# Layer 0 attention: who turns the first four heads' probabilities, and who scales k and v of the second four heads

## The chip, the cores and the metric

The kernel runs on one core of a Trainium2 chip. The metric is the device time of one execution in microseconds; three runs of the kernel before gave 2122.54, 2122.59 and 2122.71 us, median 2122.59.

Engines are named as in the profile: PE is TensorE's matmuls and PEld its weight loads, DVE is VectorE, ACT is ScalarE, POOL is GpSimd, SP is SyncE, which issues the loads from memory.

## The reference, cut to what matters

A decoder trunk of two layers over 256 tokens with a model width of 2048. Layer 0 projects the normalised input in one product to u, va, q, k and v. One half of the mixer is a gated unit with a 128x128 position mixing, the other is dilated attention with 8 heads of 128. Both halves go through one output projection. Then comes a squared-ReLU MLP; layer 1 is stick-breaking attention with 16 heads, and another MLP.

The dilated attention has three branches (window, dilation) = (128, 1), (512, 4), (2048, 16), merged by their softmax denominators:

```
s = q . k - slope(head) * distance          (causal)
p = exp(s - max(s)) * count(distance)       count = number of branches that hold this key
o = (p / sum(p)) @ v
```

With 256 tokens this is, for each head, a lower-triangular score matrix in three 128x128 blocks (queries 0-127 with keys 0-127, queries 128-255 with keys 0-127, queries 128-255 with keys 128-255).

## The kernel before

**Units and ticks.** Every large product is cut into 94 units. A unit is a product of all 256 tokens (two blocks of 128) with 512 columns of a weight matrix, over a depth of 2048: 8 ticks of two 128-deep steps each. For precision every weight is split into w_hi and w_lo and every activation likewise, so a step is three products, and a tick is 12 matmuls of 128x512 (L1203, from tick_tokens). Units 4 to 6 give q, k and v of layer 0's heads 0 to 3 (the first group), units 7 to 9 those of heads 4 to 7 (the second group), units 10 to 13 are the output projection.

**Rings.** w_raw holds the 8 ticks of a unit as they come from memory in four quarters of 1 MB. w_hi and w_lo are rings of 4 ticks. ACT makes w_hi of a tick (L394) when PE is done with the tick four before; DVE makes w_lo (L723) when w_hi is there; PE starts the tick when w_lo is there. SP issues the load of a quarter when w_lo of the ticks that lay in it is made.

**The order of the other work.** It is written out by hand. For ACT and DVE a unit is a loop over positions t = 1 to 7 and a last one: the extras of t, then the conversion of the tick four later; behind position 7 comes post (the evacuation of the unit's result), then the extras of 8 and the conversion. For PE the extras of t run ahead of tick t. Over the three units of a q, k, v group t runs from 0 to 24, and in the output projection from 0 again. Each engine executes its own list strictly in order.

**Attention of a group.** post on DVE scales q, k and v out of PSUM by the row norms (L975, scaled), into q_tok (the memory of kT), k_tok (the memory of y_sb) and v_sb; DVE turns q into qT by 16 block operations of 32x256 at the positions of TURNS_L0, and k into kT at those of TURNS_K (L829). PE's scores follow at the start of the next unit. Then, inside the next group of units: DVE adds the distances (L890), takes the maximum (t = 1, L899) and subtracts it (t = 2, L905), ACT takes the exponential (t = 3, L518), DVE multiplies by the counts (t = 4, L909) and normalises (t = 5, L914 to L918). What is left is zs, 4 heads x 384 columns, with queries on the partitions.

The values product needs the keys on the partitions, so zs has to be turned into tmp:
- first group (during units 7 to 9): at t = 8 PE transposes 12 blocks of 128x128 into PSUM (l0_pT, L1431), ACT copies them to tmp in two pieces (l0_copy_pT, L523), and PE multiplies tmp with v_sb at t = 10 (values);
- second group (during units 10 to 13): DVE turns zs in 16 block operations of 32x384, four at each of t = 6 to 9 (turn_p, L928), and PE's values run at t = 13.

After the values, ACT makes hid_hi (L527) and DVE hid_lo (L934) out of PSUM, for the output projection. PE's scores of the second group, at t = 24, wait for both and for the turned k. Semaphores: s_pn counts normalised halves, s_pT and s_pc the transposes and their copies, s_pturned the end of turn_p, s_o the values, post_done the evacuated units; PE starts unit u when units 0 to u-2 are evacuated.

Of the kernel before, what the change touches and what calls it, by code (L numbers as in the profile page):

```python
# [32 lines left out]
ACT = mybir.ActivationFunctionType  # L33
AX = mybir.AxisListType

P = 128
T = 256
TB = T // P
# [19 lines left out]
HG = 4  # L58
# [5 lines left out]
TRI = 3 * P  # L64
# [20 lines left out]

TURNS_GATE = {9: 3, 11: 2, 13: 3, 14: 4, 15: 4}
TURNS_L0 = {11: 4, 12: 4, 13: 4, 14: 4}
TURNS_L1 = {9: 2, 10: 2, 11: 4, 12: 2, 13: 4, 14: 2}
TURNS_K = {17: 4, 18: 4, 19: 4, 20: 4}

# [16 lines left out]
def trunk_kernel(nc, x_in, pre_mix, post_mix, pre_ffn, post_ffn, ab_w_in, ln_g, ln_b, sgu_w, sgu_b,  # L107
                 ab_w_out, sb_w_in, sb_w_out, ffn_w1, ffn_w2, shapes, out):
    ctx = ExitStack()
    with ctx:  # L110
# [3 lines left out]
        def sem(name):  # L114
            return ctx.enter_context(nc.semaphore(name))
# [33 lines left out]
        ident = cst[:, 0:P]  # L149
# [78 lines left out]
        s_sm = sem("s_sm")  # L228
        s_ex = sem("s_ex")
        s_pn = sem("s_pn")  # L230
        s_pT = sem("s_pT")
        s_pc = sem("s_pc")
        s_pturned = sem("s_pturned")
        s_wturned = sem("s_wturned")
        s_ab = sem("s_ab")
# [148 lines left out]
        def _(act):  # L384
# [19 lines left out]
            def unit(u, post, extras=None, first=1):  # L404

                for t in range(first, TICKS):
                    for f in (extras or {}).get(t, []):
                        f()
                    conv_at(u, t)
                post()  # L410
                for f in (extras or {}).get(TICKS, []):
                    f()
                if not (isinstance(u, int) and u == UNITS - 1):
                    conv(u + 1, 4)
# [101 lines left out]
            def l0_exp(grp):  # L516
                act.wait_ge(s_sm, 4 * grp + 4)
                nc.scalar.activation(zs[:, :, :], zs[:, :, :], ACT.Exp).then_inc(s_ex, 1)  # L518

            def l0_copy_pT(n):  # L520
                act.wait_ge(s_pT, n + 1)
                b = 2 * (n % 2)
                nc.scalar.activation(tmp[:, b:b + 2, :], ps[:, 4 + b:6 + b, 0:TRI], ACT.Copy).then_inc(s_pc, 1)  # L523

            def o_hi(n, b, tile):
                act.wait_ge(s_o, n + 1)
                nc.scalar.activation(hid_hi[:, bass.ds(tile, 2), :],  # L527
                                     ps[:, 6 + b, :].rearrange("p (h t) -> p h t", t=T), ACT.Copy).then_inc(s_ohi, 1)

            def l0_extras(grp):  # L530
                copies = {8: [lambda: l0_copy_pT(2 * grp), lambda: l0_copy_pT(2 * grp + 1)]} if grp == 0 else {}
                return {3: [lambda: l0_exp(grp)], **copies,
                        (10, 13)[grp]: [lambda: o_hi(2 * grp, 0, 8 + 4 * grp), lambda: o_hi(2 * grp + 1, 1, 8 + 4 * grp + 2)]}


            def l1_logs(b, grp):
# [23 lines left out]
                        13: [lambda: l1_weights(1, grp)],  # L560
                        15: [lambda: o_hi(2 * grp + 4, 0, 4 * grp), lambda: o_hi(2 * grp + 5, 1, 4 * grp + 2)]}

            def qkv_group(u, extras):
                for i in range(3):
                    unit(u + i, nothing, {t - 8 * i: f for t, f in extras.items() if 8 * i < t <= 8 * i + 8})

            def sum_squares_psum(u0, c):

# [120 lines left out]
            for j in range(2):  # L689
                unit(2 + j, lambda j=j: gelu_u(j))  # L690
            qkv_group(4, {t: [lambda m=m: gate_hi(m)] for m, t in enumerate(GATE_HI)})
            qkv_group(7, l0_extras(0))
            out_phase(U_OUT0, l0_extras(1), 1)
            ffn(U_FFN0, 0)

# [14 lines left out]
        def _(dve):  # L710
# [33 lines left out]
            def unit_finished(u):  # L744
                dve.wait_ge(pe_ticks, 8 * u + 8)
# [86 lines left out]
            def turns(plan, dst, src):  # L832

                at, extras = 0, {}
                for t, n in plan.items():
                    extras[t] = [lambda a=at, n=n: turn(dst, src, range(a, a + n))]
                    at += n
                return extras

            def merged(*plans):  # L840
                every = {}
                for plan in plans:
                    for t, f in plan.items():
                        every[t] = every.get(t, []) + f
                return every
# [41 lines left out]
            def l0_scores(h, head):  # L887
                dve.wait_ge(s_sc, head + 1)
                dve.wait_ge(s_cst, 16)
                nc.vector.scalar_tensor_tensor(zs[:, h, :], far_c, -(2.0 ** -(head + 1)), ps[:, 4 + h, 0:TRI],  # L890
                                               ALU.mult, ALU.add).then_inc(s_zs, 1)
# [25 lines left out]
                    m = rden[:, i, :].unsqueeze(2).broadcast_to([P, HG, z.shape[2]])  # L917
                    nc.vector.tensor_tensor(z, z, m, ALU.mult).then_inc(s_pn, 1)  # L918

            def turn_p(first):  # L920

                if first == 0:
                    dve.wait_ge(s_pn, 4)
                for n in range(first, first + 4):
                    q4, k4 = n // 4, n % 4
                    rows = zs[32 * q4:32 * q4 + 32, :, :].rearrange("p h (c k f) -> p (h c) k f", c=3, k=4)
                    cols = tmp[32 * k4:32 * k4 + 32, :, :].rearrange("p h (c q t) -> p (h c) q t", c=3, q=4)
                    last = nc.vector.transpose(cols[:, :, q4, :], rows[:, :, k4, :])  # L928
                if first == 12:
                    last.then_inc(s_pturned, 1)  # L930

            def o_lo(n, b, tile):
                dve.wait_ge(s_ohi, n + 1)
                nc.vector.tensor_tensor(hid_lo[:, bass.ds(tile, 2), :], ps[:, 6 + b, :].rearrange("p (h t) -> p h t", t=T),  # L934
                                        hid_hi[:, bass.ds(tile, 2), :].bitcast(F32), ALU.subtract).then_inc(s_olo, 1)

            def l0_extras(grp):
                return {1: [lambda: l0_max(grp)], 2: [lambda: l0_less_max(grp)], 4: [lambda: l0_count(grp)],
                        5: [lambda: l0_normalise(grp)],
                        **({t: [lambda t=t: turn_p(4 * t - 24)] for t in range(6, 10)} if grp else {}),  # L940
                        (10, 13)[grp]: [lambda: o_lo(2 * grp, 0, 8 + 4 * grp), lambda: o_lo(2 * grp + 1, 1, 8 + 4 * grp + 2)]}


            def l1_scores(h, grp):
# [22 lines left out]
                        12: [lambda: l1_exponent(1, grp)],  # L967
                        15: [lambda: o_lo(2 * grp + 4, 0, 4 * grp), lambda: o_lo(2 * grp + 5, 1, 4 * grp + 2)]}

            def qkv_group(u, extras, q_plan, scores):  # L970
                def scaled(i, dst, factor=None):

                    unit_finished(u + i)
                    for b in range(TB):
                        last = nc.vector.tensor_scalar(dst[:, b, :], ps[:, 2 * ((u + i) % 2) + b, :], rst[:, 6 + b:7 + b], factor,  # L975
                                                       ALU.mult, *(() if factor is None else (ALU.mult,)))
                    last.then_inc(post_done, 1)
                    if i < 2:
                        dve.wait_ge(post_done, u + (i + 1))

                k_turns = turns(TURNS_K, kT, k_tok)
                k_turns[20] = [lambda: turn(kT, k_tok, range(12, 16)).then_inc(s_turned, 1)]
                extras = merged(extras, turns(q_plan, qT, q_tok), k_turns,
                                {24: [lambda h=h: scores(h) for h in range(HG)]})
                for i, post in enumerate((lambda: scaled(0, q_tok, SCALE), lambda: scaled(1, k_tok),
                                          lambda: scaled(2, v_sb))):
                    unit(u + i, post, {t - 8 * i: f for t, f in extras.items() if 8 * i < t <= 8 * i + 8})
# [197 lines left out]
            gates = merged({t: [lambda m=m: gate(m)] for m, t in enumerate(GATE)},  # L1185
                           {t: [lambda m=m: gate_lo(m)] for m, t in enumerate(GATE_LO)})
            qkv_group(4, merged(turns_u(1), gates), TURNS_GATE, lambda h: l0_scores(h, h))
            qkv_group(7, l0_extras(0), TURNS_L0, lambda h: l0_scores(h, 4 + h))
            out_phase(U_OUT0, l0_extras(1), 1)
            ffn(U_FFN0, 0)  # L1190

# [9 lines left out]
        def _(pe):  # L1201
# [214 lines left out]
            def l0_scores(grp):  # L1416

                pe.wait_ge(s_turned, grp + 1)
                if grp == 0:
                    pe.wait_ge(s_sgt, 4)  # L1420
                else:
                    pe.wait_ge(s_olo, 2)
                for h in range(HG):
                    mm(ps[:, 4 + h, 0:P], qT[:, h, 0:P], kT[:, h, 0:P], True, True)
                    mm(ps[:, 4 + h, P:TRI], qT[:, h, P:T], kT[:, h, :], True, True).then_inc(s_sc, 1)

            def l0_pT(grp):
                pe.wait_ge(s_pn, 2 * grp + 2)
                for h in range(HG):
                    for c in range(3):  # L1430
                        last = nc.tensor.transpose(ps[:, 4 + h, c * P:(c + 1) * P], zs[:, h, c * P:(c + 1) * P], ident)  # L1431
                    if h % 2:
                        last.then_inc(s_pT, 1)

            def values(b, w):

                for i in range(2):
# [3 lines left out]
                last.then_inc(s_o, 1)  # L1441

            def l0_values(grp):
                pe.wait_ge(*((s_pc, 2), (s_pturned, 1))[grp])
                for b in range(2):
                    values(b, tmp[:, 2 * b:2 * b + 2, :])

            def l0_extras(grp):
                return {0: [lambda: l0_scores(grp)], **({} if grp else {8: [lambda: l0_pT(grp)]}),
                        (10, 13)[grp]: [lambda: l0_values(grp)]}  # L1450

            def l1_scores(grp):

# [159 lines left out]
```

## Time and profile before

| | |
|---|---|
| median of three runs | 2122.59 us |
| the profiled execution's own time | 2122.69 us |
| its span | 2120.7 us |
| PE busy | 2111.2 us |
| DVE busy | 1481.2 us |
| ACT busy | 1028.1 us |
| mean granted clock of TensorE | 0.999 |

The span is from the first to the last recorded instruction of one execution; 2.0 us of the execution's time lie around it. Matmuls are pipelined, so durations of PE rows overlap: the step from one start to the next is the time that a matmul costs, not its own duration. In a timeline row the first number is the start, the second the time covered by the instructions that the row merges.

### The profile page before, as it was taken

The numbers are of one execution on the slowest core, as the hardware profiler recorded it, in microseconds if no ns is written. First come the engines' busy times: TensorE is split into PE (matmuls) and PEld (weight loads), VectorE is DVE, ScalarE is ACT, GpSimd is POOL, SyncE is SP. The second block draws the span as 40 slices with busy tenths as digits, with TensorE's granted clock in tenths as the row PEclk, the third lists the DMA queues.
The fourth block names the chain that finished last, engine by engine and source line by source line (L and its number), as shares of the span: only waits on it lengthen the run. The fifth ranks groups of instructions, "written<-read, shape, count | busy, mean of one in ns | idle before, by whom it ended". The sixth has DMA issues, their size and how long they took to land.

```text
span 2120.7 us, 25442 instructions
## 1 busy us (share of the span) xinstructions
PE 2111.2 (100%) x9448; PEld 1748.5 (82%) x9448; DVE 1481.2 (70%) x1924; ACT 1028.1 (48%) x1180; POOL 20.1 (1%) x24
## 2 busy tenths in 40 slices
PE   9999999999999999999999999999999999999998
PEld 7888888888888888888888888888888888888886
DVE  6797867764774775586778778577746855764875
ACT  6444346543543453454645554665434544544553
POOL 0000001000000000000000000000000000000000
PEclk9999999999999999999999999999999999999999
DMA  9655555656656656655555555456556566656553
GB/s 323 207 179 171 191 193 170 206 195 187 195 199 190 186 198 218 184 193 198 178 179 178 179 178 199 160 160 216 199 186 192 180 213 182 198 197 214 183 199 119
DMA packets 204077, 406.81 MB, mean 192 GB/s; under 512 B 6544, under 2 KB 9936, under 8 KB 203472
## 3 DMA queue, kind: packets, MB, share of 16 engines
q1 hardware_dynamic: 203712, 405.37, 58.3%
q8 instruction: 63, 1.03, 0.2%
q14 instruction: 30, 0.25, 0.0%
q10 hardware_dynamic: 272, 0.16, 0.0%
HBM read 403.41 MB, written 2.10 MB: 191 GB/s over the span
## 4 chain that ended last, share of the span: by engine, by line
PE 99%; DVE 0%; DVEq 0%; ACT 0%; issue 0%; POOL 0%; POOLq 0%
PE ps L1203 99%; PE ps L1352 1%; DVE x_sb L767 0%; PE ps L1431 0%; DVE act_pair L1111 0%; DVE act_pair L773 0%; ACT tmp L497 0%; DVE y_sb L1081 0%; DVEq L110 0%; DVE w_lo L800 0%; PE ps L1257 0%; POOL rs_bc L350 0%; PE ps L1545 0%; PE ps L1550 0%; DVE rst L856 0%
## 5 line engine op out<-in xcount | busy, mean ns | idle before, releaser
L723 DVE TENSOR_TENSOR w_lo<-w_raw,w_hi 128x1024 fp32r<-128x1024 f32 x750 | 910.7, 1225 | 561.9 <-ACT w_hi L394 558.2
L394 ACT ACTIVATE w_hi<-w_raw 128x1024 fp32r<-128x1024 f32 x750 | 789.9, 1061 | 897.0 <-PE ps L1203 893.2
L1203 PE MATMUL ps<-w_hi,act_pair 128*128 128x512 f32 x3456 | 1072.0, 390 | 0.4 <-ACT w_hi L457 0.3
L1203 PEld LDWEIGHTS ps<-w_hi,act_pair 128*128 128x128 f32 x3456 | 647.1, 188 | 136.2 <-issue 2.0
L1203 PE MATMUL ps<-w_lo,act_pair 128*128 128x512 f32 x1728 | 670.2, 390 | 0.0
L1203 PE MATMUL ps<-w_hi,hid_hi 128*128 128x512 f32 x1280 | 498.7, 390 | 0.0
L1203 PE MATMUL ps<-w_hi,hid_lo 128*128 128x512 f32 x1280 | 498.0, 389 | 0.0
L1203 PE MATMUL ps<-w_lo,hid_hi 128*128 128x512 f32 x1280 | 498.0, 389 | 0.0
L1203 PEld LDWEIGHTS ps<-w_lo,act_pair 128*128 128x128 f32 x1728 | 324.1, 188 | 66.6 <-DVE w_lo L800 0.4
L829 DVE STREAM_TRANSPOSE qT<-kT 32x256 f32<-32x256 f32 x608 | 265.0, 436 | 42.2 <-ACT kT L605 32.8
L1203 PEld LDWEIGHTS ps<-w_hi,hid_lo 128*128 128x128 f32 x1280 | 240.2, 188 | 50.0
L1203 PEld LDWEIGHTS ps<-w_hi,hid_hi 128*128 128x128 f32 x1280 | 240.3, 188 | 49.7
L1203 PEld LDWEIGHTS ps<-w_lo,hid_hi 128*128 128x128 f32 x1280 | 240.3, 188 | 49.5
L610 ACT ACTIVATE hid_hi<-qT 128x512 fp32r<-128x512 f32 x64 | 37.0, 627 | 124.2 <-DVE qT L829 124.2
L829 DVE STREAM_TRANSPOSE kT<-y_sb 32x256 f32<-32x256 f32 x96 | 41.8, 435 | 1.6
L1033 DVE TENSOR_TENSOR hid_lo<-qT,hid_hi 128x512 fp32r<-128x512 f32 x64 | 41.2, 685 | 0.0
L601 ACT ACTIVATE qT<-ps,rst 128x512 f32<-128x512 f32 x64 | 40.1, 676 | 0.0
L605 ACT ACTIVATE kT<-qT 128x1024 f32<-128x1024 f32 x32 | 34.0, 1062 | 1.0
L425 ACT ACTIVATE act_pair<-ps,gpre 128x256 fp32r<-128x256 f32 (+1 forms) x80 | 28.3, 450 | 8.2 <-PE ps L1352 8.1
L364 POOL TENSOR_TENSOR rst<-rst,neg_half 128x1 f32<-128x1 f32 (+1 forms) x13 | 11.1, 855 | 2093.3 <-DVE rst L856 1994.8
L773 DVE SCALAR_TENSOR_TENSOR act_pair<-ps,gpre,act_pair 128x256 fp32r<-128x256 f32 (+1 forms) x70 | 28.2, 460 | 1.5 <-ACT act_pair L425 1.3
L497 ACT ACTIVATE tmp<-ps 128x512 f32<-128x512 f32 x20 | 11.9, 593 | 30.7 <-PE ps L1203 22.8
(104 smaller groups left out, 474.3 us busy)
## 6 DMA issues: line engine op xcount, KB each, us to landing
w_raw<-in_ffn_w_dram SPq DMA_DIRECT2D x256, 1024.0 KB, 5.3
w_raw<-in_sb_w_in_dram SPq DMA_DIRECT2D x48, 1024.0 KB, 5.1
w_raw<-in_ab_w_in_dram SPq DMA_DIRECT2D x36, 1024.0 KB, 5.2
w_raw<-in_ab_w_out_dram SPq DMA_DIRECT2D x16, 1024.0 KB, 5.0
w_raw<-in_sb_w_out_dram SPq DMA_DIRECT2D x16, 1024.0 KB, 5.0
w_raw<-in_ab_w_in_dram SPq DMA_DIRECT2D x6, 512.0 KB, 8.5
x_sb<-in_x_dram SPq DMA_DIRECT2D x8, 256.0 KB, 7.2
gpost<-in_norm_post_mix_dram SPq DMA_DIRECT2D x2, 1024.0 KB, 7.9
```

The lines of the kernel that those rows point to most:

```text
L394: nc.scalar.activation(w_hi[:, t % RING, :, :], w_raw[:, t // 2, h:h + 2, :], ACT.Copy).then_inc(hi_ready, 1)
L425: last = nc.scalar.activation(act_hi[:, kt, part], ps[:, x_bank(k, j), i * T + part.start:i * T + part.stop], ACT.Copy, scale=gpre[:, k * ...
L497: nc.scalar.activation(junk[:, 2 * NC:3 * NC], src, ACT.Square, accum_out=ssy[:, b, c:c + 1]).then_inc(s_ssy, 1)
L601: last = nc.scalar.activation(relu_tok[:, b, :], ps[:, 2 * (j % 2) + b, :], ACT.Relu, scale=rst[:, 6 + b:7 + b])
L605: nc.scalar.activation(sq_tok, relu_tok, ACT.Square).then_inc(f_sq, 1)
L610: nc.scalar.activation(hid_hi[:, 4 * j + i:4 * j + i + 2, :], sq_T[:, i:i + 2, :], ACT.Copy).then_inc(f_hi, 1)
L723: nc.vector.tensor_tensor(w_lo[:, t % RING, :, :], w_raw[:, t // 2, h:h + 2, :], w_hi[:, t % RING, :, :].bitcast(F32), ALU.subtract).then_ ...
L773: last = nc.vector.scalar_tensor_tensor(act_lo[:, kt, part], ps[:, x_bank(k, i if k == 0 and j == 0 else j), i * T + part.start:i * T + pa ...
L829: last = nc.vector.transpose(cols[:, :, :, tp, :], rows[:, :, :, fq, :])
L1033: nc.vector.tensor_tensor(hid_lo[:, tiles, :], sq_T[:, i:i + 2, :], hid_hi[:, tiles, :].bitcast(F32), ALU.subtract).then_inc(done, 1)
L1203: return nc.tensor.matmul(dst, lhsT, rhs, start=start, stop=stop, skip_group_check=True)
L1352: last = nc.tensor.transpose(ps[:, x_bank(k, j), i * T + b * P:i * T + (b + 1) * P], x_sb[:, b, kt * P:(kt + 1) * P], ident)
```

## The change

For the first group the PE transposes, the ACT copies and their two semaphores are gone. DVE's turn_p gets the group as an argument and does the job in both groups: in the first with two block operations at each of t = 6 to 13. PE's values, ACT's hid_hi and DVE's hid_lo of the first group move from t = 10 to t = 15.

The turns of the second group's q move with it: before, four at each of t = 11 to 14; now two at 11 and 12 and four at 13, 14 and 15, and DVE waits for the end of the last.

k and v of the second group (units 8 and 9) are scaled out of PSUM by ACT instead of DVE, two activations of 128x512 each. DVE waits at its own place of post for k only. q stays with DVE, and so do all three in the other groups.

```diff
+TURNS_L0_LATE = {11: 2, 12: 2, 13: 4, 14: 4, 15: 4}
+VALUES_L0 = (15, 13)
...
 ACT
-            def l0_copy_pT(n):
-                act.wait_ge(s_pT, n + 1)
-                b = 2 * (n % 2)
-                nc.scalar.activation(tmp[:, b:b + 2, :], ps[:, 4 + b:6 + b, 0:TRI], ACT.Copy).then_inc(s_pc, 1)
...
+            def scaled(u, dst):
+                unit_finished(u)
+                act.wait_ge(post_done, u)
+                for b in range(TB):
+                    last = nc.scalar.activation(dst[:, b, :], ps[:, 2 * (u % 2) + b, :], ACT.Copy, scale=rst[:, 6 + b:7 + b])
+                last.then_inc(post_done, 1)
...
-            qkv_group(7, l0_extras(0))
+            qkv_group(7, l0_extras(0), (nothing, lambda: scaled(8, k_tok), lambda: scaled(9, v_sb)))
...
 DVE
-            def turn_p(first):
+            def turn_p(grp, first, end):
                 if first == 0:
-                    dve.wait_ge(s_pn, 4)
-                for n in range(first, first + 4):
+                    dve.wait_ge(s_pn, 2 * grp + 2)
+                for n in range(first, end):
...
-                        **({t: [lambda t=t: turn_p(4 * t - 24)] for t in range(6, 10)} if grp else {}),
-                        (10, 13)[grp]: [lambda: o_lo(...), lambda: o_lo(...)]}
+                        **({t: [lambda t=t: turn_p(1, 4 * t - 24, 4 * t - 20)] for t in range(6, 10)} if grp else
+                           {t: [lambda t=t: turn_p(0, 2 * t - 12, 2 * t - 10)] for t in range(6, 14)}),
+                        VALUES_L0[grp]: [lambda: o_lo(...), lambda: o_lo(...)]}
...
+                    if i in by_act:
+                        if i < 2:
+                            dve.wait_ge(post_done, u + (i + 1))
+                        return
...
+                if by_act:
+                    q_turns[15] = [lambda: chain(turn(qT, q_tok, range(12, 16)))]
...
-            qkv_group(7, l0_extras(0), TURNS_L0, lambda h: l0_scores(h, 4 + h))
+            qkv_group(7, l0_extras(0), TURNS_L0_LATE, lambda h: l0_scores(h, 4 + h), (1, 2))
...
 PE
-            def l0_pT(grp):
-                pe.wait_ge(s_pn, 2 * grp + 2)
-                for h in range(HG):
-                    for c in range(3):
-                        last = nc.tensor.transpose(ps[:, 4 + h, c * P:(c + 1) * P], zs[:, h, c * P:(c + 1) * P], ident)
-                    if h % 2:
-                        last.then_inc(s_pT, 1)
...
             def l0_values(grp):
-                pe.wait_ge(*((s_pc, 2), (s_pturned, 1))[grp])
+                pe.wait_ge(s_pturned, grp + 1)
...
-                return {0: [lambda: l0_scores(grp)], **({} if grp else {8: [lambda: l0_pT(grp)]}),
-                        (10, 13)[grp]: [lambda: l0_values(grp)]}
+                return {0: [lambda: l0_scores(grp)],
+                        VALUES_L0[grp]: [lambda: l0_values(grp)]}
```

## Rows read from the trace of the kernel before

**Rows 1.** The page's part 1: busy us, share of the span, instructions.

```profile
PE 2111.2 (100%) x9448; PEld 1748.5 (82%) x9448; DVE 1481.2 (70%) x1924; ACT 1028.1 (48%) x1180; POOL 20.1 (1%) x24
```

**Rows 2.** The chain that ended last: start us, us, what.

```profile
45.74 145.22 PE ps L1203 x660
190.95 1.31 PE ps L1431 x12
192.26 137.15 PE ps L1203 x618
```

**Rows 3.** Timeline of PE and PEld, 189 to 201: start us, us, instruction.

```profile
190.79 1.47 PE L1431 MATMUL ps<-cst,zs 128*128 128x128 f32 x12
192.02 0.48 PE L1203 MATMUL ps<-w_hi,act_pair 128*128 128x512 f32 x1
192.10 0.19 PEld L1203 LDWEIGHTS ps<-w_lo,act_pair 128*128 128x128 f32 x1
...
197.59 2.78 PE L1203 MATMUL ps<-tmp,v_sb 128*128 128x256 f32 x16
200.13 0.48 PE L1203 MATMUL ps<-w_hi,act_pair 128*128 128x512 f32 x1
```

**Rows 4.** Timeline of ACT, 191 to 218, with idle time before and releaser.

```profile
191.05 1.06 ACT L394 ACTIVATE w_hi<-w_raw 128x1024 fp32r<-128x1024 f32 x1 [1.66 <-PE ps L1203]
...
205.92 1.06 ACT L394 ACTIVATE w_hi<-w_raw 128x1024 fp32r<-128x1024 f32 x1 [1.66 <-PE ps L1203]
208.64 1.06 ACT L394 ACTIVATE w_hi<-w_raw 128x1024 fp32r<-128x1024 f32 x1 [1.66 <-PE ps L1203]
...
216.80 1.06 ACT L394 ACTIVATE w_hi<-w_raw 128x1024 fp32r<-128x1024 f32 x1 [1.66 <-PE ps L1203]
```

**Rows 5.** Timeline of DVE, 190 to 211.

```profile
190.31 3.49 DVE L723 TENSOR_TENSOR w_lo<-w_raw,w_hi 128x1024 fp32r<-128x1024 f32 x3
193.72 1.41 DVE L975 TENSOR_SCALAR kT<-ps,rst 128x512 f32<-128x512 f32 x2
...
205.44 1.77 DVE L829 STREAM_TRANSPOSE qT<-kT 32x256 f32<-32x256 f32 x4
...
208.48 1.78 DVE L829 STREAM_TRANSPOSE qT<-kT 32x256 f32<-32x256 f32 x4
```

**Rows 6.** One line's instructions, ACT: a scaled activation, min/median/max ns.

```profile
L601 ACT ACTIVATE qT<-ps,rst x64: 671/677/682, 357.6 to 2027.3; 128x512 f32<-128x512 f32 x64
```

**Rows 7.** Timeline of DVE, 264 to 276, and the line's min/median/max ns.

```profile
264.81 1.23 DVE L723 TENSOR_TENSOR w_lo<-w_raw,w_hi 128x1024 fp32r<-128x1024 f32 x1
266.07 2.31 DVE L928 STREAM_TRANSPOSE tmp<-zs 32x384 f32<-32x384 f32 x4
...
273.24 2.33 DVE L928 STREAM_TRANSPOSE tmp<-zs 32x384 f32<-32x384 f32 x4
...
L928 DVE STREAM_TRANSPOSE tmp<-zs x16: 560/570/574, 262.5 to 275.0; 32x384 f32<-32x384 f32 x16
```

**Rows 8.** Timeline of the opening, 1 to 7.

```profile
1.17 2.93 PE L1203 MATMUL ps<-rs_bc 128*128 128x256 f32 x6 [1.17 <-POOL rs_bc L350]
...
5.59 0.68 DVE L800 TENSOR_TENSOR w_lo<-w_raw,w_hi 128x512 fp32r<-128x512 f32 x1
6.33 0.30 PEld L1203 LDWEIGHTS ps<-w_lo,act_pair 128*128 128x128 f32 x2 [0.41 <-DVE w_lo L800]
```

**Rows 9.** Timeline of DVE at the start of unit 10.

```profile
245.01 1.23 DVE L723 TENSOR_TENSOR w_lo<-w_raw,w_hi 128x1024 fp32r<-128x1024 f32 x1 [0.96 <-ACT w_hi L394]
```

**Rows 10.** Timeline of PE, the second group's values.

```profile
276.30 2.78 PE L1203 MATMUL ps<-tmp,v_sb 128*128 128x256 f32 x16
```

**Rows 11.** DMA issues: count, KB each, median us from issue to landing.

```profile
w_raw<-in_ab_w_in_dram SPq DMA_DIRECT2D x36, 1024.0 KB, 5.2
```

**Rows 12.** Stretches after the last matmul: busy us by engine, PEclk, DMA share, GB/s.

```profile
2112.90:2117.00 4.10, 0.00 (x0) 0.00 (x0) 3.32 (x7) 0.52 (x2) 0.54 (x1) 1.00 0.32 132
2117.00:2120.70 3.70, 0.00 (x0) 0.00 (x0) 0.36 (x1) 0.00 (x0) 0.00 (x0) 0.50 0.69 256
```

More of the change, by code:

```diff
@@ L230, in trunk_kernel @@
         s_pn = sem("s_pn")
-        s_pT = sem("s_pT")
-        s_pc = sem("s_pc")
         s_pturned = sem("s_pturned")
@@ L530, in l0_extras @@
             def l0_extras(grp):
-                copies = {8: [lambda: l0_copy_pT(2 * grp), lambda: l0_copy_pT(2 * grp + 1)]} if grp == 0 else {}
-                return {3: [lambda: l0_exp(grp)], **copies,
-                        (10, 13)[grp]: [lambda: o_hi(2 * grp, 0, 8 + 4 * grp), lambda: o_hi(2 * grp + 1, 1, 8 + 4 * grp + 2)]}
+                return {3: [lambda: l0_exp(grp)],
+                        VALUES_L0[grp]: [lambda: o_hi(2 * grp, 0, 8 + 4 * grp), lambda: o_hi(2 * grp + 1, 1, 8 + 4 * grp + 2)]}
             def l1_logs(b, grp):
@@ L561, in l1_extras, with qkv_group @@
                         15: [lambda: o_hi(2 * grp + 4, 0, 4 * grp), lambda: o_hi(2 * grp + 5, 1, 4 * grp + 2)]}
-            def qkv_group(u, extras):
+            def scaled(u, dst):
[4 more added lines that the diff above has]
+                last.then_inc(post_done, 1)
+            def qkv_group(u, extras, posts=(nothing, nothing, nothing)):
                 for i in range(3):
-                    unit(u + i, nothing, {t - 8 * i: f for t, f in extras.items() if 8 * i < t <= 8 * i + 8})
+                    unit(u + i, posts[i], {t - 8 * i: f for t, f in extras.items() if 8 * i < t <= 8 * i + 8})
             def sum_squares_psum(u0, c):
@@ L928, in turn_p @@
                     last = nc.vector.transpose(cols[:, :, q4, :], rows[:, :, k4, :])
-                if first == 12:
+                if end == 16:
                     last.then_inc(s_pturned, 1)
@@ L939, in l0_extras @@
                         5: [lambda: l0_normalise(grp)],
-                        **({t: [lambda t=t: turn_p(4 * t - 24)] for t in range(6, 10)} if grp else {}),
-                        (10, 13)[grp]: [lambda: o_lo(2 * grp, 0, 8 + 4 * grp), lambda: o_lo(2 * grp + 1, 1, 8 + 4 * grp + 2)]}
+                        **({t: [lambda t=t: turn_p(1, 4 * t - 24, 4 * t - 20)] for t in range(6, 10)} if grp else
+                           {t: [lambda t=t: turn_p(0, 2 * t - 12, 2 * t - 10)] for t in range(6, 14)}),
+                        VALUES_L0[grp]: [lambda: o_lo(2 * grp, 0, 8 + 4 * grp), lambda: o_lo(2 * grp + 1, 1, 8 + 4 * grp + 2)]}
             def l1_scores(h, grp):
@@ L968, in l1_extras, with qkv_group @@
                         15: [lambda: o_lo(2 * grp + 4, 0, 4 * grp), lambda: o_lo(2 * grp + 5, 1, 4 * grp + 2)]}
-            def qkv_group(u, extras, q_plan, scores):
+            def qkv_group(u, extras, q_plan, scores, by_act=()):
                 def scaled(i, dst, factor=None):
+                    if i in by_act:
+                        if i < 2:
+                            dve.wait_ge(post_done, u + (i + 1))
+                        return
                     unit_finished(u + i)
@@ L982, in qkv_group @@
                 k_turns[20] = [lambda: turn(kT, k_tok, range(12, 16)).then_inc(s_turned, 1)]
-                extras = merged(extras, turns(q_plan, qT, q_tok), k_turns,
+                q_turns = turns(q_plan, qT, q_tok)
+                if by_act:
+                    q_turns[15] = [lambda: chain(turn(qT, q_tok, range(12, 16)))]
+                extras = merged(extras, q_turns, k_turns,
                                 {24: [lambda h=h: scores(h) for h in range(HG)]})
```

## The prediction

> **What bounds the kernel now.** I read the page's busy shares first: PE is busy 2111.2 us of a span of 2120.7 us, VectorE (DVE) 70%, ScalarE (ACT) 48% [rows 1]. Then the chain of waits. It is PE nearly from end to end, and around the change it is 145.22 us of matmuls, then the twelve transposes for 1.31 us, then 137.15 us of matmuls, with no wait between them [rows 2]. So any time that PE spends or loses in this stretch moves the end one for one, and what DVE and ACT do costs nothing as long as PE never waits for it. The last view is the timeline of each engine around 190 us, for how early DVE is with what PE needs next.
>
> I count ticks of the second group (heads 4 to 7 being projected) from 0. PE ends tick 7 at 190.79, turns the probabilities, does ticks 8 and 9, and starts the values products at 197.59 [rows 3]. A tick is 2.72 us: the starts of ACT's conversions, each released by the end of a tick, lie that far apart [rows 4]. DVE's work is in one strict order of positions: before position t come the extras of t, then the conversion of w_lo for tick t+4. It came out of the normalising late: position 5's conversion starts at 190.31, and those of 5, 6 and 7 run back to back [rows 5], though the last of their three w_hi had been there since 192.11 [rows 4] and the others a tick and two earlier. DVE therefore starts the changed stretch with a backlog.
>
> **What goes from PE.** The transposes hold PE 190.79 to 192.02. The two ticks behind them take until 197.59, that is 5.57 us where two at the usual pace are 5.44 us. Without them the values products' old place comes at 190.79 + 5.44 = 196.23 instead of 197.59: 1.36 us less. ACT loses the two copies of tmp; it waits 1.66 us for PE in a tick anyway [rows 4], so this is worth nothing.
>
> **What DVE gets, and when PE needs it.** Sixteen block transposes of 32x384, two ahead of each position 6 to 13, and the values wait for the last. The same operation on the same tiles stands in the next group: four take 2.31 to 2.33 us, 0.58 us each, and the conversion behind takes 1.26 us until the next transpose [rows 7]. The other pieces: a conversion followed by something else 1.14 us, the scaling of q 1.41 us plus some 0.06 us for the wait on itself, four turns of q with the conversion behind them 3.04 us, so 1.78 us for four turns [rows 5]. DVE's queue from 190.31 to the last transpose:
> - eight conversions (positions 5 to 12): two at 1.14 (5 and 7) and six at 1.26, 9.8 us
> - the scaling of q: 1.5 us
> - sixteen transposes: 9.3 us
> - the two plus two turns of q planned at 11 and 12: 1.8 us
>
> Together 22.4 us: the last transpose ends at 212.7. Nothing in this list waits for ACT or PE: the conversion of position 8 would start at 198.8, and its w_hi is there by 194.8 (tick 8 ends 193.51, and ACT needs 1.3 us); each later one has more room.
>
> PE, undisturbed, ends tick 14 at 190.79 + 7 x 2.72 = 209.83 and stands before the values of position 15. It is released at 212.7 + 0.06: in the opening a load of weights starts 0.06 us after the DVE instruction it waits for [rows 8]. The first load of weights is then not hidden behind a matmul: two in a row took 0.30 us, one shows as 0.19 us [rows 3, 8], so the next step comes after 0.11 us; I put 0.1 us for it (0 to 0.2). **PE stands still for 3.0 us** (2.7 to 3.3 with the pieces' scatter), in a place where it now never does.
>
> Ticks up to 14 don't wait first. PE needs w_lo of tick 12 at 201.67 and it is ready at 200.1; of tick 13 at 204.39, ready 202.5; of tick 14 at 207.11, ready 204.9; margins 1.6, 1.9 and 2.2 us. And if one of them did fail, that wait would come out of the later one, since the release of the values hangs on DVE's queue alone.
>
> **Behind the stall.** Values 2.54 us as now, then tick 15 ends at 218.2 (now 216.5, from ACT's conversion at 216.80 [rows 4]). Queued on DVE behind the last transpose: four turns of q, conversion 13 (done 215.7; tick 17 wants it at 220.9), four turns, conversion 14 (done 218.7, wanted 223.7), the two hid_lo and four turns with the wait on itself, conversion 15 (done 223.1, wanted 226.4). DVE catches up while PE stands.
>
> ACT's scaling of k costs two activations; the same form elsewhere is 677 ns [rows 6], so k_tok is there some 2.7 us after tick 15, at 220.9. DVE, which waits for it before position 16, gets there at 223.1: no time. Behind DVE's wait stand the k turns and conversion 16; the k turns end near 235.3, and the scores need them at 239.9. ACT has 1.66 us a tick free and nothing of PE's next three ticks hangs on it. The scaling of v goes the same way; DVE loses 1.4 us of it, then waits for ACT's conversion anyway, as it does now at 245.01, where the idle time before it is 0.96 us [rows 9]. So the second group's values, whose last transpose now ends 0.7 us before PE asks (275.57 against 276.30 [rows 7, 10]), keep that margin: both move with PE. I cost both scalings at nothing; if that cover failed they would cost up to 1.4 us each. SP's load for ticks T and T+1 is released by the w_lo of tick T-7, made at position T-11, and ACT wants it at position T-4: 7 x 2.72 = 19 us, against 5.2 us to land [rows 11]; a DVE that is some 5 us late leaves that room. The wait after the last turns of q is a wait of DVE on itself of 0.06 us, under the same cover.
>
> **The sum.** -1.36 + 3.0 = +1.6 us. The profiled execution took 2122.69 us, 0.10 above the median of the runs, so 2122.59 + 1.6 = 2124.2 us.
>
> **Two rules of the Trainium skill.** By the rows, a transpose costs PE 0.11 us (1.31 us for twelve), and DVE 9.3 us for the whole job. "VectorE: DVE Perf Modes", section "Rules for kernel authors", says to turn 128x128 blocks on TensorE if a PSUM destination will do, which speaks against this change. In its section "The three transpose paths" a TensorE transpose is 390 ns; by that the change would free 4.7 us of PE and end 1.7 us faster. No chance goes to that result: the rows price these very transposes, pipelined at 0.11 us, and the forecast comes out on the rule's side for another reason, DVE's backlog.
>
> At the end, in the stretch from 2112.9 on in which no matmul runs, the granted clock holds 1.00 for 4.1 us and is 0.50 after that: from 2.4 to 1.2 GHz [rows 12]. "TensorE: Matmul & The Clock Gate", section "What's actually happening", has the low level as the default, which activity releases. The trace agrees; whether 3.0 us of standing still is enough for it, no row shows. It is the first rival.
>
> **Rivals.**
> 1. The stall also lowers the clock. For: PE stops for 3 us, which it nowhere does between its first ticks and its last. Against: the clock held for 4.1 us at the end. If it fell for the values and nothing more, their 2.54 us would double, 2126.7 us; with the tick behind them too, 2129.5 us. A row with such a price is the opening, where six matmuls of 256 columns took 2.93 us, 0.49 us each [rows 8]; in the values, eight of 128 and eight of 256 columns in 2.54 us, one of 256 is some 0.21 us.
> 2. The other side: DVE is in time, PE doesn't wait, and the whole 1.36 us stay: 2121.2 us. Its place is the release of the values at 209.8. The queue would have to fit 19.5 us instead of 22.4, so a transpose would have to cost 0.40 us instead of 0.58; from 0.49 us down the change is no loss. Against it: all sixteen in the trace took 560 to 574 ns [rows 7], and even the smaller 32x256 turns 0.44 us.
> 3. A second wait behind the first: DVE, with the twelve turns and two hid_lo ahead of the k turns, is late with conversion 14 or 15, or with the k turns. The margins are 5.0, 3.3 and 4.6 us, so it needs an unseen delay of over 3 us; a loss of 1 to 2 us on top, 2125.7 us.
> 4. That the change doesn't do what it says: if the compiled order kept DVE's work elsewhere, the transposes would still be gone from PE, and it is the second rival's time.
>
> **How the numbers follow.** Forecast (stall at full clock) 0.76, own range 2123.7 to 2124.8; lower clock 0.10; no or less stall than gain 0.09; second wait 0.05. The range from 2121.2 to 2126.0 takes in the forecast, the second wait and the no-stall case, and leaves out the lower clock. What a measurement of this kernel tells from no change is 0.2%, 4.2 us. Slower by more than that means above 2126.8: half of the first rival and a little of the third, 0.06. Faster by that, below 2118.3, no case gives: 0.01. Same: 0.93.
>
> **What would show it.** In the changed trace PE idles once, for some 3 us, just before the products of tmp and v_sb near 210 us, with DVE's transpose named as the releaser; DVE is busy without a gap from 190.3 to 212.7; tick 14 ends at 209.8; the granted clock is 1.00 throughout; there is no other PE idle time, and everything behind lies 1.6 us later than now. I am wrong if PE's idle time there is under 1.3 us, if w_lo holds PE at tick 12 to 14, or if the clock column drops behind the stall.

## The result

Over seven runs each the changed kernel takes 2130.7 us (2129.09 to 2131.19) and the kernel before 2122.71 us (2122.49 to 2123.16); the ratio is 1.0035, 95% interval 1.0025 to 1.0045. It is slower by 8.0 us where 1.6 were forecast, and the time lies outside the range. The profiled execution took 2130.98 us, span 2129.0 us, mean granted clock 0.997.

The runs fall into two groups: three from 2129.1 to 2129.6 us with a mean clock of 0.998, four from 2130.7 to 2131.2 us with 0.997. The distance, some 1.5 us, is about what one of the two low clocks below costs; that the three runs had one of them and not both is inferred, since one execution alone was traced.

The page's busy row, and its row of the queue that loads instructions (packets, MB, share of time). In the kernel before that queue has 63 packets and 1.03 MB.

```profile
PE 2113.9 (99%) x9436; PEld 1750.2 (82%) x9436; DVE 1487.3 (70%) x1936; ACT 1027.4 (48%) x1182; POOL 20.0 (1%) x24
q8 instruction: 72, 1.18, 0.2%
```

PE's waits: engine, who released it, us in total, times, longest.

```profile
PE ps L1213 <- issue: 2.9, 1, 2.9
PE ps L1213 <- DVE tmp L930: 2.7, 1, 2.7
PE ps L1213 <- POOL rs_bc L350: 1.2, 1, 1.2
PE ps L1213 <- DVE w_lo L802: 0.2, 1, 0.2
```

The wait for tmp is the forecast one. The first row was in no forecast: PE stood still for 2.9 us and, by the profile, waited for nobody. Where each lies, in the timelines of DVE around 212 and of PE around 212 and in the MLP of layer 1:

```profile
211.83 1.16 DVE L930 STREAM_TRANSPOSE tmp<-zs 32x384 f32<-32x384 f32 x2
213.02 1.78 DVE L831 STREAM_TRANSPOSE qT<-kT 32x256 f32<-32x256 f32 x4
```

```profile
209.93 0.39 PE L1213 MATMUL ps<-w_hi,act_pair 128*128 128x512 f32 x1
213.05 4.55 PE L1213 MATMUL ps<-tmp,v_sb 128*128 128x256 f32 x16 [2.73 <-DVE tmp L930]
217.35 0.48 PE L1213 MATMUL ps<-w_hi,act_pair 128*128 128x512 f32 x1
...
1767.99 0.42 PE L1213 MATMUL ps<-w_hi,act_pair 128*128 128x512 f32 x1
...
1769.17 0.40 PE L1213 MATMUL ps<-w_hi,act_pair 128*128 128x512 f32 x1
1772.48 0.39 PE L1213 MATMUL ps<-w_hi,act_pair 128*128 128x512 f32 x1 [2.92 <-issue]
```

The values products are issued over 213.05 to 217.35, 4.30 us where the kernel before has 2.54 [rows 3]. The stretches around both stops say why; the column behind POOL is the granted clock, as a share of 2.4 GHz.

```profile
210.50:213.00 2.50, 0.00 (x0) 0.00 (x0) 2.44 (x4) 0.97 (x1) 0.00 (x0) 1.00 1.02 388
213.00:216.40 3.40, 3.35 (x10) 2.90 (x11) 3.29 (x6) 0.39 (x1) 0.00 (x0) 0.51 0.73 308
216.40:220.00 3.60, 3.60 (x20) 3.08 (x19) 3.54 (x7) 0.81 (x2) 0.00 (x0) 0.99 0.73 244
1769.60:1772.40 2.80, 0.00 (x0) 0.00 (x0) 0.96 (x1) 0.00 (x0) 0.00 (x0) 1.00 0.41 92
1772.90:1776.30 3.40, 3.40 (x9) 2.62 (x9) 0.34 (x1) 1.06 (x1) 0.00 (x0) 0.51 0.75 272
```

In the 3.4 us behind each stop the clock is at 0.51, the lower of its two levels (1.2 of 2.4 GHz), and PE loses about half of that. So the 8.3 us between the two profiled executions are, term by term: -1.36 for the transposes; +0.33 for the opening (the end of tick 14 is at 210.16 instead of 209.83; the same point of the opening, the small transpose near 45 us, moves by up to 0.9 us from kernel to kernel, 45.46 to 46.33 us in the ten traces without padding at the start); +2.9 for the wait; +1.75 for the slow values; +2.92 for the second stop; +1.7 for its low clock. The sum is 8.2.

### The profile page after: what moved, and what is told of

Same layout as the page of the kernel before. It is cut to its first block, busy times and chain, and to the rows that moved or that the text cites. A ratio compares the mean times of both kernels' runs of the same rounds, so it can differ in the third digit from the quotient of the medians.

```text
span 2129.0 us, 25434 instructions
## 1 busy us (share of the span) xinstructions
PE 2113.9 (99%) x9436; PEld 1750.2 (82%) x9436; DVE 1487.3 (70%) x1936; ACT 1027.4 (48%) x1182; POOL 20.0 (1%) x24
## 4 chain that ended last, share of the span: by engine, by line
PE 96%; DVE 2%; SPq 1%; DMA 1%; issue 0%; ACT 0%; DVEq 0%; ACTq 0%
PE ps L1213 96%; DVE w_lo L725 1%; DMA w_raw<-in_ab_w_in_dram 1%; PE ps L1362 1%; DVE tmp L930 0%; SPq L309 0%; SPq L299 0%; SPq L322 0%; ACT w_hi L394 0%; DVE x_sb L769 0%; DVE den L916 0%; DVE zs L920 0%; SPq L304 0%; DVE qT L831 0%; DVE zs L911 0%
```

## The experiments

Two things had to be explained. For the first stop: is the low clock a consequence of PE's standing still? For the second, some words on the code ahead. Each layer's MLP is written with a loop (`pe.Fori`), whose body of some 1,600 PE instructions runs twice from the same place of PE's instruction stream; `1767.99` above is the first matmul of the second pass in layer 1. Theory A was that the place of a loop in PE's instruction stream decides, because the change took 24 PE instructions out ahead of it; the rival was anything else that the change shifted in time. The kernel before gave 2122.70 us beside the first four kernels (31 runs, 2122.47 to 2123.84) and 2122.84 us beside the next four (27 runs, 2122.37 to 2123.61).

**pad24**: the stream behind 213 us back at its old place.

```diff
             def l0_values(grp):
+                if grp == 0:
+                    for _ in range(24):
+                        pe.sem_inc(s_pad, 1)
                 pe.wait_ge(s_pturned, grp + 1)
```

> The changed kernel, with 24 semaphore increments (of a semaphore that nobody reads) in PE's stream just ahead of the first group's wait for the turned probabilities. They run inside that wait, and every PE instruction behind them lies at the same place of the stream as in the kernel before (the change took 24 instructions out: 12 loads of weights and 12 matmuls). Theory A (PE's second stop, 2.92 us at 1769.6 with nothing waited for, comes from where the MLP loop of layer 1 lies in PE's instruction stream): that stop is gone, and the low clock behind it; what is left is -1.36 + 2.9 + 1.7 (clock behind the first stop) + up to 0.3, 2126.0 to 2126.3 us, and PE idles only at 210 to 213. Rival (the stop comes from something else that the change shifted, such as transfers or the other engines' code): still 2129.1 to 2131.2 us with the stop near 1769.6.

2125.95 us in the median of ten runs. PE's waits, the page's row of the instruction queue, and the clock behind the stop:

```profile
PE ps L1214 <- DVE tmp L931: 2.7, 1, 2.7
PE ps L1214 <- POOL rs_bc L351: 1.2, 1, 1.2
PE ps L1214 <- DVE w_lo L726: 0.2, 1, 0.2
```

```profile
q8 instruction: 63, 1.03, 0.2%
```

```profile
213.00:216.40 3.40, 3.19 (x12) 2.77 (x13) 3.28 (x7) 0.60 (x1) 0.00 (x0) 0.64 0.82 342
216.40:220.00 3.60, 3.60 (x17) 2.98 (x17) 3.54 (x7) 0.60 (x1) 0.00 (x0) 0.86 0.66 242
```

The second stop and the nine additional instruction loads are gone; 4.75 us come back with them. What is left of the change is the first stop, and the runs differ in their clock: three at 2124.5 to 2124.8 us with a mean clock of 0.999, five at 2125.6 to 2126.3 with 0.998, two at 2127.2 and 2127.3 with 0.997. The traced execution is one of the five, and in it the low clock is seen; for the others it is inferred from time and mean clock. So the same stop of 2.7 us lowers the clock in most executions and not in all. The last two lose some 2.6 us against the first three, more than the 1.75 us that were traced, and neither was traced.

**filler**: PE has matmuls to do while it waits.

```diff
+                if grp == 0:
+                    for _ in range(12):
+                        mm(ps[:, 6, :], act_pair[:, 0, 0, 0:P], act_pair[:, 0, :, :], True, True)
                 pe.wait_ge(s_pturned, grp + 1)
```

> The changed kernel, with 12 matmuls of 128x512 into an unused PSUM bank ahead of the same wait: 12 x 0.227 = 2.7 us of PE work where it otherwise stands still, and again 24 instructions, so the stream behind lies as before. Theory A: PE's wait shrinks to some 0.2 us, the values products start at the same 213.0, the granted clock stays 1.00, no stop near 1769: 2122.7 - 1.36 + 2.9 = 2124.3 us (to 2124.6), 1.7 us less than pad24. Rival (the clock falls whatever PE does there, or the slow values products have another cause): the same as pad24, 2126.

2124.41 us, and all ten runs between 2124.12 and 2124.98. PE's timeline, and the stretches as above:

```profile
210.55 2.88 PE L1213 MATMUL ps<-act_pair 128*128 128x512 f32 x12
213.45 2.89 PE L1213 MATMUL ps<-tmp,v_sb 128*128 128x256 f32 x16
```

```profile
210.50:213.00 2.50, 2.50 (x12) 2.07 (x12) 2.43 (x5) 1.06 (x1) 0.00 (x0) 1.00 0.93 323
213.00:216.40 3.40, 3.38 (x19) 2.71 (x19) 3.31 (x6) 0.63 (x2) 0.00 (x0) 1.00 0.91 374
```

DVE is as late as before and the values start no earlier, but the clock stays at 1.00 and the time is 1.5 us below pad24's median. The 12 matmuls also put the stream behind them back at its old place, as in pad24, and no second stop appears (63 packets). So the 1.5 us are the price of the clock alone, and the low clock is a consequence of PE having nothing to do.

**values17**: the wait removed by asking later.

```diff
-VALUES_L0 = (15, 13)
+VALUES_L0 = (17, 13)
```

> The changed kernel with the first group's values, hid_hi and hid_lo at t = 17 instead of 15. PE comes there two ticks later, at about 215.5, and the last transpose is over at 213.0. Theory A: no wait there and no low clock there; the transposes' 1.36 us are gained; the stop in the MLP of layer 1 stays (2.9 us, and 1.7 us of low clock behind it in some executions): 2124.3 to 2126.0 us. Rival (that stop comes from the timing of transfers or other engines, which shifts here by over 4 us): 2121.3 us.

2125.99 us (2123.96 to 2126.43). PE's waits no longer have tmp in them; the second stop is as long as it was, though it lies 5 us earlier. Behind this stop, too, the clock falls in some executions only: three runs take 2124.0 to 2124.7 us with a mean clock of 0.999 (the traced one is among them and holds 1.00 there), seven 2125.7 to 2126.4 us with 0.998. Its waits and its instruction queue:

```profile
PE ps L1213 <- issue: 2.9, 1, 2.9
PE ps L1213 <- POOL rs_bc L350: 1.2, 1, 1.2
PE ps L1213 <- DVE w_lo L802: 0.3, 1, 0.3
```

```profile
q8 instruction: 72, 1.18, 0.2%
```

**no_transposes**: the kernel before, and only PE's stream shorter.

```diff
-                for h in range(HG):
-                    for c in range(3):
-                        last = nc.tensor.transpose(...)
-                    if h % 2:
-                        last.then_inc(s_pT, 1)
+                for h in range(2):
+                    pe.sem_inc(s_pT, 1)
```

> The kernel before without the 12 transposes on PE (two semaphore increments in their place; ACT copies what lies in PSUM, so the first group's probabilities are left out of the result). DVE, ACT and all places are as before; only PE's stream is 23 instructions shorter behind 190 us. Theory A: the transposes' 1.36 us are gained, and the stop in the MLP of layer 1 appears: 2122.7 - 1.36 + 2.9 = 2124.3 us, 2126.0 where the clock falls behind it. Rival: 2121.3 us and no stop.

2125.96 us (2124.42 to 2126.89): with PE work taken away and everything else in its place, the kernel, which leaves the first group's probabilities out of its result, is 3.3 us slower. The timeline at the stop:

```profile
1764.22 0.19 PEld L1203 LDWEIGHTS ps<-w_hi,act_pair 128*128 128x128 f32 x1
1764.44 0.39 PE L1203 MATMUL ps<-w_hi,act_pair 128*128 128x512 f32 x1
1767.58 0.19 PEld L1203 LDWEIGHTS ps<-w_hi,act_pair 128*128 128x128 f32 x1 [3.18 <-issue]
1767.59 0.50 PE L1203 MATMUL ps<-w_hi,act_pair 128*128 128x512 f32 x1 [2.75 <-issue]
```

The instruction queue has 72 packets again. Here the seventh load of weights of the loop's pass waits; in the changed kernel, whose stream is one instruction shorter here, the seventh load had run and its matmul waited. Counted in the compiled stream, both are instruction 13043.

**values17_pad8**: is it that place?

```diff
+                if grp == 0:
+                    for _ in range(8):
+                        pe.sem_inc(s_pad, 1)
```

> As values17, with 8 increments ahead of the values. Counted in the compiled stream of PE, the stop so far came in front of one and the same instruction, number 13043: the matmul of the seventh product behind the loop's start in the changed kernel, and the load of weights of the seventh in no_transposes, whose stream is one instruction longer. With 8 more, number 13043 is the matmul of the third product. Theory A, fixed place of the stream: the stop of 2.9 us now comes behind two matmuls of the loop's second pass, not behind six. Rival (the stop hangs on the loop's start, or on time): behind six matmuls, or no stop. Time 2124 to 2127 us either way with a stop.

2127.77 us, one run. The timeline:

```profile
1763.89 0.40 PE L1214 MATMUL ps<-w_hi,act_pair 128*128 128x512 f32 x1
1764.13 0.40 PE L1214 MATMUL ps<-w_lo,act_pair 128*128 128x512 f32 x1
1764.13 0.19 PEld L1214 LDWEIGHTS ps<-w_hi,act_pair 128*128 128x128 f32 x1
...
1768.29 0.62 PE L1214 MATMUL ps<-w_hi,act_pair 128*128 128x512 f32 x2 [3.76 <-issue]
```

Two matmuls and the third load run, the third matmul waits: number 13043 again. The stop is longer, 3.8 us, where 2.9 were expected. The rows say why: PE goes on 4.4 us behind the pass's first matmul (1763.89 to 1768.29) here and 4.5 us behind it in the changed kernel (1767.99 to 1772.48), so with two products ahead of the place instead of six less work lies inside that time. In both traces a packet of the instruction queue starts 2.1 to 2.2 us behind the pass's first matmul and takes 1.0 us, that is, inside the stop.

**before_pad100, before_pad150, before_pad180**: the kernel before, its whole PE stream moved.

```diff
+            for _ in range(100):            # or 150, or 180
+                pe.sem_inc(s_pad, 1)
             pe.wait_ge(s_warm, 1)
```

> The kernel before, with 100 semaphore increments at the start of PE's stream; nothing else. The stops so far came in front of instruction 13043, and the profile shows PE's instructions loaded in pieces of 16,384 bytes, 256 instructions. Theory A in full: the pieces begin at numbers that leave 243 when divided by 256; a loop that touches 7 of them is run in its second pass without loading, one that touches 8 is not and PE stops once. Here layer 0's MLP loop (4810 to 6419) touches 8 and layer 1's 7: a stop of 3 to 4 us with nothing waited for in the loop of layer 0, in front of number 4851, some 18 products behind the second pass's start, near 687 us; none in layer 1. Rival (it hangs on the loop's start lying just ahead of a piece, or on layer 1's loop alone): no stop.

> As before_pad100 with 150. Both loops touch 7 pieces (4860 to 6469, 13200 to 14809): no stop, 2122.7 us plus what 150 increments cost in the opening (0 to 3 us). Rival (any shift of the stream brings a stop): one near 687 or 1772.

> As before_pad100 with 180. Layer 0's loop touches 7 pieces, layer 1's (13230 to 14839) reaches into an eighth with its end: a stop of 3 to 4 us in layer 1's loop, in front of number 13299, some 33 products behind the second pass's start, near 1772 us; none in layer 0. Rival (only a start just ahead of a piece matters): no stop.

One run each: 2137.75, 2145.09 and 2150.83 us. At the very start an increment costs PE 0.16 us, where no matmul runs ahead of it (16.1 us of waiting for 100, 23.8 for 150, 28.4 for 180), so the opening carries most of these times, and the stops have to be read in the trace. PE's waits and the instruction queue of the three, in this order:

```profile
PE ps L1204 <- issue: 16.4, 2, 16.1
```

```profile
q8 instruction: 72, 1.18, 0.2%
```

```profile
PE ps L1204 <- issue: 23.8, 1, 23.8
```

```profile
q8 instruction: 63, 1.03, 0.2%
```

```profile
PE ps L1204 <- issue: 29.3, 2, 28.4
```

```profile
q8 instruction: 73, 1.20, 0.2%
```

Which loop loads again came out as expected in all three: 100 gives nine more loads, in layer 0's loop for the first time (packets start at 694, 699 and 705 us there, and none between 1756 and 1957 us in layer 1's); 150 gives none; 180 gives ten more, in layer 1's. The sizes were missed, and once the place. The two stops, the first with the first matmul of its pass:

```profile
697.39 0.45 PE L1204 MATMUL ps<-w_hi,act_pair 128*128 128x512 f32 x1
...
701.71 0.73 PE L1204 MATMUL ps<-w_hi,act_pair 128*128 128x512 f32 x2 [0.22 <-issue]
```

```profile
1792.49 0.49 PE L1204 MATMUL ps<-w_hi,act_pair 128*128 128x512 f32 x1 [0.90 <-issue]
```

The first is behind some 18 products, as expected (687 us plus 15 us of opening), but 0.2 us long, not 3 to 4. That fits the two stops above: PE goes on 4.3 us behind the pass's first matmul (697.39 to 701.71), and by then 18 products, some 4.1 us of work, have hidden nearly all of it. The forecast of 3 to 4 us had left this work out. The second is 0.9 us long and lies at the start of the pass, not 33 products into it. So in these traces the number of pieces tells whether the loop loads again. Where the loop starts ahead of a piece's border, the stop in these three is some 4.4 us less the work between the pass's start and that border; for a loop whose end reaches into the eighth piece I have no rule.

**q_late_pad24**: a shorter first stop. Besides what is shown, it has pad24's 24 increments.

```diff
-TURNS_L0_LATE = {11: 2, 12: 2, 13: 4, 14: 4, 15: 4}
+TURNS_L0_LATE = {13: 4, 14: 4, 15: 4, 16: 4}
...
-                    q_turns[15] = [lambda: chain(turn(qT, q_tok, range(12, 16)))]
+                    q_turns[16] = [lambda: chain(turn(qT, q_tok, range(12, 16)))]
```

> As pad24, with q's turns of the second group at 13, 14, 15 and 16, four each; so none of them lies ahead of the last transpose. The release comes 4 x 0.44 = 1.8 us earlier, near 211.2, and PE stands still for some 1.2 us instead of 2.9. Theory: -1.36 + 1.2 and up to 0.3 for the opening: 2122.5 to 2122.9 us; and the clock holds in every execution, so that 1.7 us of a shorter wait bring 3.2 us against pad24's median. Rival (a short stop lowers the clock too): 2124.2 us in some executions.

2122.59 us (2122.46 to 2123.39); PE's wait and the clock in it and behind it:

```profile
211.06 2.88 PE L1214 MATMUL ps<-tmp,v_sb 128*128 128x256 f32 x16 [0.93 <-DVE tmp L931]
```

```profile
210.20:211.05 0.85, 0.00 (x0) 0.00 (x0) 0.81 (x3) 0.83 (x1) 0.00 (x0) 1.00 1.03 393
211.10:216.00 4.90, 4.90 (x26) 4.32 (x27) 4.76 (x10) 1.38 (x3) 0.00 (x0) 1.00 0.85 304
```

A wait shorter by 1.8 us brings 3.4 us against pad24's median, because no execution pays for the clock, by their times and mean clocks (0.999 in all ten).

**act_scales**: the second half of the change alone. Shown is the call on ACT; its `scaled` and DVE's side are as in the change, with the turns of q at their old places.

```diff
-            qkv_group(7, l0_extras(0))
+            qkv_group(7, l0_extras(0), (nothing, lambda: scaled(8, k_tok), lambda: scaled(9, v_sb)))
```

> The kernel before with ACT instead of DVE scaling k and v of the second group, and nothing else: PE's stream is unchanged. Both theories: no difference, 2122.5 to 2122.9 us; DVE loses 2.8 us of work in a place where it waits for ACT anyway, and ACT has 1.66 us a tick free. If the scaling held something up, PE would idle near 213 to 245.

2123.08 us (2122.79 to 2123.84) against 2122.84: 0.24 us more, ratio 1.0001 with the interval 0.9992 to 1.0010. PE's only wait is the opening's, and the opening of its profiled execution is 0.8 us longer than in the kernel before. No effect that can be told.

**values17_pad24**: both repairs, that is, values17's edit and pad24's.

> Both repairs: the first group's values at t = 17, and 24 semaphore increments of PE ahead of their wait (now not hidden in a wait; some 0.03 us each or less, up to 0.7 us). Theory: no PE idle time at either place, granted clock 1.00 to the end, 2122.7 - 1.36 = 2121.3 us plus what the increments cost, 2121.3 to 2122.1, and all executions within some 0.5 us. Rival (the two stops hid something else that is late): 2123 or more.

2121.53 us (2121.14 to 2121.98, eleven runs), 1.3 us below the kernel before; the ratio is 0.9994, interval 0.9985 to 1.0003, but no run of the one reaches into the runs of the other (2122.37 and up). PE's one wait:

```profile
PE ps L1214 <- POOL rs_bc L351: 1.2, 1, 1.2
```

It is the only version whose runs all lie below those of both kernels (q_late_pad24's median of 2122.59 us is within the scatter of the kernel before). What it gains is the transposes' 1.36 us: the two traced spans differ by 1.2 us (2119.5 against 2120.7), with an opening that is 0.2 us longer here. The 24 increments cost 0.1 us: from the first values product to the next matmul it is 2.61 us (215.46 to 218.07), and 2.53 us in values17.

## Why the prediction was wrong

**Right, by its own steps.** DVE is busy without a gap from 190.64 on, and the last transpose ends at 212.99; forecast 212.7, and the 0.3 us are the opening's. PE ends tick 14 at 210.16 (209.83) and stands still until 213.05, 2.9 us (3.0). values17_pad24 gives back the transposes' 1.36 us. The scalings by ACT and the moved turns of q and k cost nothing (act_scales; PE has no wait between 218 and 1769), and the second group's values keep their margin: last transpose over at 279.19, PE there at 279.93, 0.7 us as before [rows 7, 10]. No tick in this stretch waited for w_lo. Had only this happened, the time would be filler's: 2124.4 us, against the forecast of 2124.2.

**The step that failed first: "Forecast (stall at full clock) 0.76 ... lower clock 0.10".** The rival was named, at the right place, and its chance was wrong; the clock column drops behind the stall, which the prediction gave as a sign of being wrong. I held the end of the trace against it, where the clock stayed at 1.00 for 4.1 us behind 2112.9 [rows 12]. The runs show that this proves nothing for a stop in the middle: a stop of 2.7 us lowered the clock in seven of ten runs of pad24, one of 2.9 us in seven of ten of values17, and one of 0.9 us in none of ten of q_late_pad24. So the same stop falls on either side from run to run, and one example of a clock that held was no bound. By the Trainium skill, page "TensorE: Matmul & The Clock Gate", section "HAM oscillation — how this bites in real kernels", a kernel whose PE waits some 3 to 5 us for data between its bursts of matmuls comes back at the low clock every time. The stops here are a little shorter and agree with it in most executions, not in all. The price of the low clock, 1.5 us between the medians and 1.75 us in the trace, was below the 2.5 us that I took, since it ended before the values products did. This step alone would have left pad24's 2125.95 us, just inside the range; that it is inside is luck.

**The step that was missing, and that put the time outside the range: "there is no other PE idle time, and everything behind lies 1.6 us later than now".** It took the code behind the change for untouched. But 24 instructions fewer on PE moved the rest of its stream, and the MLP loop of layer 1 (some 1,600 instructions) came to lie across eight pieces of 16 KB instead of seven. It then loads instructions again in its second pass, PE stops for 2.92 us in front of instruction 13043, and the clock may fall behind that stop too (1.7 us in the trace). pad24 takes it away, no_transposes brings it about with nothing else changed, values17_pad8 and no_transposes fix the place to the instruction, and the three shifts of the kernel before move it to layer 0's loop, away, and back to layer 1's. It costs 4.75 us of the 8.0 (after against pad24). The rival of a second wait, 0.05, was for a late DVE and had nothing of this.

Together: -1.4 + 2.9 + 1.5 (clock, median) for the part that was looked at, 4.75 for the one that was not, 0.3 for the opening of the traced execution: 8.1, against the measured 8.0.

**Left open.** That the loads belong to PE and that seven pieces fit and eight don't is worked out from their number, size and gaps: with seven pieces there is no load for some 200 us, the second pass (1751 to 1955 us in the kernel before); with eight there are four within 17 us around its start (1759 to 1776 us in the changed kernel) and more behind. Each of the three shifts of the kernel before, and values17_pad8, was run once. What decides in which execution a stop of 2.8 us lowers the clock was not tried.

## What to carry to other kernels

Where an engine is never idle, ask of every moved result whether it will be there on time, with the whole queue of the engine that makes it; and count the clock on top of a stop of PE: behind one of 2.7 to 2.9 us it came to some 1.5 to 1.75 us more here in most executions, behind one of 0.9 us nothing. When a long unrolled stream with a loop changes by a few instructions, compare the packets of the instruction queue and look for idle time that nobody released before explaining anything: an unrelated loop may have moved across a border, and here 24 harmless instructions put it back. A planned wait can be filled or avoided (two ticks later cost nothing here), and only with both repairs was the edit worth its 1.3 us.

## What was not expected of the hardware

- Removing work from the busiest engine made the kernel slower (no_transposes, +3.3 us), through a stop of 2.8 us while instructions were loaded and, in most executions, the low clock behind it.
- A loop of some 1,600 PE instructions runs its second pass without a load (63 packets) or with nine or ten more (72, 73), by where it begins; the stop was 0.2, 0.9, 2.9 and 3.8 us in four places. In three of them PE went on 4.3 to 4.5 us behind the pass's first matmul.
- 24 semaphore increments ahead of the values cost 0.1 us together while PE is busy (values17_pad24), and the same instruction 0.16 us each at the start, where nothing runs (16.1 us for 100).
